# Laying the attention of two transformer layers between the projection units, in groups of two heads

## The reference

```python
xn = rms_norm(h, norm_mix[i]);  mn = rms_norm(mem, norm_mem[i])
mk, mv = halves(mn @ w_mem_kv[i])                  # 4 memory heads
q, k, v, (f_logit), qm = parts(xn @ w_in[i])       # 12 heads of 64; f_logit in layer 0 only
# layer 0 (fox):  s = q.k/8 + F[t] - F[s], F = cumsum(log_sigmoid(f_logit + b)), causal
# layer 1 (moba): one block of 256, so s = q.k/8 - slope[h]*(t-s), causal
# memory heads:   s = qm.mk/8 over 256 memory rows, no mask
h = h + concat(softmax(s) @ v for all 16 heads) @ w_out[i]
h = h + (silu(hn @ w_gate) * (hn @ w_up)) @ w_down[i]     # hn = rms_norm(h, norm_ffn[i]), width 2816
```

## Time and profile before

| | us |
|---|---|
| median of 3 runs | 1815.13 (1812.03 to 1815.88) |
| profiled execution, own time | 1809.4 |
| its span, first to last instruction | 1807.7 |
| TensorE busy | 1595.3 (88%) |
| VectorE busy | 1018.7 (56%) |
| ScalarE busy | 726.1 (40%) |
| mean granted clock of TensorE | 0.932 |

### The profile page before, as it was taken

One profiled execution on the slowest core, in us unless ns is written; L12 is line 12 of the kernel. 1 busy time (PEld: TensorE's weight loads), 2 busy tenths in 40 slices (PEclk: granted clock), 3 DMA queues, 4 the chain that ended last, 5 costly groups with the idle time before them and its releaser, 6 DMA issues.

```text
span 1807.7 us, 23290 instructions
## 1 busy us (share of the span) xinstructions
PE 1595.3 (88%) x7836; PEld 1144.4 (63%) x7836; DVE 1018.7 (56%) x2272; ACT 726.1 (40%) x1750; POOL 513.4 (28%) x573
## 2 busy tenths in 40 slices
PE   5999999999899899997999997888887778777776
PEld 4975789998865799996888786444442223222222
DVE  4443476666654566663335315666666667666644
ACT  4543354444343444443154201434444444444432
POOL 1000000000100000000000001777777776777773
PEclk9975899999975899998999899999999999999999
DMA  7420247664730256662433233999999999999997
GB/s 282 165 92 1 71 152 254 239 249 152 255 118 1 94 198 244 244 220 76 144 110 119 70 140 118 411 410 409 409 409 409 409 409 409 410 409 409 409 410 285
DMA packets 102017, 443.97 MB, mean 246 GB/s; under 512 B 11376, under 2 KB 11648, under 8 KB 84272
## 3 DMA queue, kind: packets, MB, share of 16 engines
q0 software_dynamic: 81632, 297.80, 42.0%
q1 hardware_dynamic: 19584, 141.57, 21.5%
q10 hardware_dynamic: 720, 3.59, 0.5%
HBM read 441.86 MB, written 1.05 MB: 245 GB/s over the span
## 4 chain that ended last, share of the span: by engine, by line
PE 58%; DMA 22%; POOL 9%; DVE 4%; issue 4%; ACT 2%; ACTq 0%; POOLq 0%; DVEq 0%
DMA late<-expert_v,idx 18%; PE PS L400 12%; PE PS L413 7%; PE PS L418 7%; PE PS L422 7%; POOL attn L348 5%; POOL late L356 5%; PE PS L709 4%; PE PS L516 4%; PE PS L489 3%; PE PS L449 3%; PE PS L552 2%; PE PS L556 2%; PE PS L557 2%; DMA attn<-expert_u,idx 2%
## 5 line engine op out<-in xcount | busy, mean ns | idle before, releaser
L709 PE MATMUL PS<-late,wrg 128*128 128x512 f32 x1024 | 500.2, 616 | 130.6 <-DMA late<-expert_v,idx 114.5
L709 PEld LDWEIGHTS PS<-late,wrg 128*128 128x128 f32 x1024 | 177.5, 190 | 439.1 <-DMA late<-expert_v,idx 276.6
L1545 DVE CUSTOM_DVE_ANT_0 attn<-attn,PS 128x1024 f32<-128x1024 f32 x256 | 312.5, 1221 | 238.3 <-DMA attn<-expert_u,idx 238.3
L348 POOL DMA_INDIRECT attn<-expert_u,idx x256 | 241.4, 943 | 380.8 <-DVE idx L1529 300.5
L356 POOL DMA_INDIRECT late<-expert_v,idx x256 | 241.4, 943 | 98.5 <-PE PS L709 54.3
L334 POOL DMA_DIRECT2D ada<-w_ada x46 | 24.4, 530 | 734.2 <-DVE mod L1155 734.2
L1067 DVE TENSOR_TENSOR early_splits<-ring,early_splits 128x1024 fp32r<-128x1024 f32 x132 | 161.6, 1225 | 98.4 <-ACT early_splits L771 92.3
L771 ACT ACTIVATE early_splits<-ring 128x1024 fp32r<-128x1024 f32 x132 | 139.4, 1057 | 150.6 <-PE PS L413 104.2
L400 PE MATMUL PS<-XN,ring 128*128 128x256 f32 x816 | 183.8, 386 | 15.6 <-DVE XN L1376 7.8
L400 PEld LDWEIGHTS PS<-XN,ring 128*128 128x128 f32 x816 | 158.0, 194 | 42.8 <-DVE XN L1376 8.2
L1013 ACT ACTIVATE gel<-dot 128x1 f32<-128x1 f32 x256 | 51.3, 200 | 283.6 <-DVE dot L1545 283.1
(11 more groups left out here) (245 smaller groups left out, 2341.8 us busy)
## 6 DMA issues: line engine op xcount, KB each, us to landing
ring<-wstream SPq DMA_DIRECT2D x134, 1024.0 KB, 4.8
ada<-w_ada POOLq DMA_DIRECT2D x48, 512.0 KB, 3.9
attn<-expert_u,idx POOLq DMA_INDIRECT x256, 17.7
late<-expert_v,idx POOLq DMA_INDIRECT x256, 17.7
con<-const ACTq DMA_DIRECT2D x1, 1168.0 KB, 11.9
MEM<-mem_t ACTq DMA_DIRECT2D x1, 1024.0 KB, 7.7
X<-x_t ACTq DMA_DIRECT2D x1, 1024.0 KB, 9.6
subk<-sub_keys POOLq DMA_DIRECT2D x1, 1024.0 KB, 7.5
```

Of the source, the lines that this page charges most:

```text
L348: gp.indirect_dma_start(UB[i % SLOTS_U], None, expert_u, bass.IndirectOffsetOnAxis(ap=idx[:, n % 3, k:k + 1], axis=0)).then_inc(u_landed[i ...
L709: mm = pe.matmul(PS[:, 2 * b + g, :], DIAG[:, i % 8, :], VB[i % SLOTS_V][:, g * 512:(g + 1) * 512], start=n % 8 == 0 and k == 0, stop=n % ...
L1545: ve.tensor_tensor_reduce(row, row, H2N[n // 8], 1.0, 0.0, ALU.mult, ALU.add, dot[:, n % 2, k:k + 1]).then_inc(dot_ready, 1)
```

## The change

- Order of the units (SP): the stream in HBM stays, but units are loaded singly, in the order of `FUSED`: memory queries, q0, k0, v, then q, k and v in turns, then the output units. A load waits for the unit six before it.
- Attention in 16 groups of two heads and one block of queries. After the projection unit of a step TensorE turns the group before, does the scores of this group, and multiplies the one before with V. The memory heads come first. Both heads' scores lie in banks 4 and 5, both turned parts in bank 6, heads in bank 7. Some steps (`v` units, the last output units) have no new group.
- VectorE does the softmax of the group before it splits the next unit; one maximum and one inversion serve both heads; memory scores aren't copied, the maximum and the exponential read PSUM. The heads' low part is made group by group.
- The first three output units multiply the first six pairs of heads (18 of 24 matmuls), then the last two pairs as these come.
- The sum of squares of X of layer 0 is made at the start; in layer 1 after the first memory key unit, with the other three behind it. The memory split for layer 1 is spread over the feed forward.
- `ada_sum` runs 36 times in feed forward 0 (two a step), 12 times in feed forward 1, never in the projections; `trig` moves to feed forward 1. The residual adds after a feed forward begin as pairs of chunks end (`down_part`). Dummy activations load ScalarE's tables ahead of their use.
- Two small weight loads (wrg, wig) move from the start to the end of feed forward 1.

```diff
+FUSED = (("qm", 0, 0), ("qm", 1, 1), ("q", 0, 1), ("k", 0, 1), ("v", 0, 1), ("v", 1, 0),
+         ("q", 1, 1), ("k", 1, 1), ("q", 2, 1), ("k", 2, 1), ("v", 2, 0), ("v", 3, 0),
+         ("q", 3, 1), ("k", 3, 1), ("q", 4, 1), ("k", 4, 1), ("v", 4, 0), ("v", 5, 0),
+         ("q", 5, 1), ("k", 5, 1), ("wo", 0, 1), ("wo", 1, 1)) + tuple(("wo", c, 0) for c in range(2, KC))
+PAIR_ORDER = (6, 7, 0, 1, 2, 3, 4, 5)
+HELD = 3
+EARLY = 6
 # tensor
+            def group_scores(layer, g):
...
+                for hh, r in enumerate(rows):
+                    mm = pe.matmul(PS[:, 4 + hh, 0:nk], QT[r, pair, b * P:(b + 1) * P], KT[r, pair, 0:nk],
+                                   start=True, stop=not fox)
...
+                        mm = pe.matmul(PS[:, 4 + hh, 0:nk], con[r, c0:c0 + P], FT[r, 0:nk], start=False, stop=True)
+            def attend(layer, before, now):
+                if before is not None:
+                    group_turn(layer, before)
+                if now is not None:
+                    group_scores(layer, now)
+                if before is not None:
+                    group_values(layer, before)
...
+                proj(bank["km", 0], at, mem, (mh_ready, ml_ready))
+                if layer:
+                    norm_sum(NORM_BANK, SQ, KC)
+                proj(bank["km", 1], at + 1, mem)
+                pair_half(bank["vm", 1], at + 2, 0, mem)
+                pair_half(bank["vm", 1], at + 3, 1, mem)
...
+                for s, (kind, c, _) in enumerate(FUSED[:-KC]):
+                    u = FUSED_AT[layer] + s
...
+                    attend(layer, before, group_at[s])
+                    before = group_at[s]
...
+                for c in range(HELD):
...
+                    out_part(bank["wo", c], u, PAIR_ORDER[:EARLY], first=True, signal=c == 0)
+                    attend(layer, before, group_at[s])
 # vector, one step of first_block
+                    if before is not None:
+                        group_tops(layer, before)
+                    if earlier is not None:
+                        group_low(layer, earlier)
+                    if before is not None:
+                        group_normalise(layer, before)
+                    split_lo(FUSED_AT[layer] + s + 2)
 # scalar, one step
+                    if before is not None:
+                        group_exps(layer, before)
+                    split_hi(FUSED_AT[layer] + s + 2)
...
+                        take(KT[:, c, :], tile("k", c))
...
+                    if before is not None:
+                        group_turned(layer, before)
+                        group_heads(layer, before)
 # vector, start of layer 0
+            split_lo(0)
+            chunks_lo(MEML, MN, MEMH, mh_ready, ml_ready)
+            split_lo(1)
+            invert_rms()
+            scale_norm(XN, X, gain("norm_mix0"), RS, normed)
```

More of the change, by code:

```diff
@@ L337, in _ @@
             gp.wait_ge(down_done, 2 * NF)
[L338 removed]
+            for dst, src in ((wuq, w_uq), (wukv, w_ukv), (wrg[:], w_rg), (wig[:], w_ig)):
                 gp.dma_start(dst, src).then_inc(latent_loaded, 16)
@@ new lines, in group_turn @@
+            def group_turn(layer, g):
+                pair, b = groups[g]
+                nk, base = keys_of(pair, b), len(groups) * layer
+                pe.wait_ge(p_ready, base + g + 1)
+                if g >= 1:
+                    pe.wait_ge(pt_copied, base + g)
+                out, probs = halves(6, nk), two(PR, g, nk)
+                for hh in range(2):
+                    for kc in range(nk // P):
+                        mm = pe.transpose(out[:, hh, kc * P:(kc + 1) * P], probs[:, hh, kc * P:(kc + 1) * P], ident)
+                mm.then_inc(pt_ready, 1)
@@ new lines, in group_values @@
+            def group_values(layer, g):
+                pair, b = groups[g]
+                nk, base = keys_of(pair, b), len(groups) * layer
+                pe.wait_ge(pt_copied, base + g + 1)
+                if g >= 1:
+                    pe.wait_ge(heads_lo, base + g)
+                nkc, turned = nk // P, two(PT, g, nk)
+                for hh in range(2):
+                    h = 2 * pair + hh
+                    for kc in range(nkc):
+                        mm = pe.matmul(PS[DH * hh:DH * hh + DH, 7, 0:P], V[:, kc, h * DH:(h + 1) * DH],
+                                       turned[:, hh, kc * P:(kc + 1) * P], start=(kc == 0), stop=(kc == nkc - 1))
+                mm.then_inc(pv_done, 1)
@@ new lines, in group_normalise @@
+            def group_normalise(layer, g):
+                pair, b = groups[g]
+                nk, base = keys_of(pair, b), len(groups) * layer
+                a = 2 * (g % 2)
+                ve.wait_ge(exp_done, base + g + 1)
+                ve.reciprocal(rsum[:, a:a + 2], ssum[:, a:a + 2]).then_inc(vec_step, one(vec_step))
+                ve.wait_ge(vec_step, own(vec_step))
+                probs = two(PR, g, nk)
+                for hh in range(2):
+                    ins = ve.tensor_scalar(probs[:, hh, :], probs[:, hh, :], rsum[:, a + hh:a + hh + 1], None, ALU.mult)
+                ins.then_inc(p_ready, 1)
@@ L1188, in feed_forward @@
                 product_lo(1, 1, False)
+                if layer == 0:
+                    scale_norm(MN, MEM, gain("norm_mem1"), RM, mem_normed, range(4, KC))
+                    ve.wait_ge(c_ready, due(c_ready))
+                else:
+                    trig(0, 1)
                 u += 5
+                loops = (NF - 4) // 2
                 steps = own(vec_step)
[L1191 to L1199 removed]
@@ new lines, in feed_forward @@
+                u += 3 * (NF - 4)
+                for f in (NF - 2, NF - 1):
+                    split_lo(u)
+                    split_lo(u + 1)
+                    product(f, f % 2, True)
+                    split_lo(u + 2)
+                    product_lo(f, f % 2, True)
+                    if layer == 0:
+                        half = KC // 2 * (f % 2)
+                        chunks_lo(MEML, MN, MEMH, mh_ready, ml_ready, range(half, half + KC // 2))
+                    else:
+                        trig(1, f % 2)
+                    u += 3
```

883 lines of the change are left out of this document (511 added, 372 removed).

## The result

The changed kernel took **1817.94 us** (median; 1815.54 to 1821.26), the kernel before 1809.23 (1803.41 to 1815.88) on the same chip: ratio **1.0043**, 95% interval 1.0032 to 1.0054. It is 0.4% slower; 1712 was forecast, in a range of 1688 to 1772. The profiled execution took 1816.62 us, its span is 1815.0, against 1809.4 and 1807.7.

The account below looks back on a forecast made before the run. Low-clock TensorE was taken to bound attention. Gains of 3.6 + 45.4 + 6.1 + 49.8 + 0.5 less 2 make 103.4; 1809.4 - 103.4 = 1706, plus 5.7 gives 1712 us, range 1688 to 1772.

Parts of the forecast that it names:

- What bounds the kernel: Attention stages, 89.48 and 74.29 us: bound by TensorE at its lower level, 1.2 GHz, mean clock 0.54.
- The rival with a low clock in the pieces: Fused stages: clock low in attention pieces, units at full speed; 1776 us; chance 0.16, fully or in part.
- the one that loses by it: Fused stages: low clock takes the 55 units too, 5.1 in place of 2.88 us each; 1898 us; chance 0.04.
- Layer 0: Start wins 3.6 us (0 to 6); from there to the norm 130.6 against 176.0 us, 45.4 won.
- Attention between units: Attention pieces between projection units, at full clock: 40 us in layer 0, 34 us in layer 1.
- New waits: Fused stages: TensorE waits for softmax and PSUM copies, 8.5 us a layer, plus 1.5 for layer 0's table loads.
- Layer 1: Start wins 6.1 us (3 to 7); then 120.3 against 170.1 us, 49.8 won.
- What is moved into the feed forward: Feed forward 0: one more ada_sum a step fits VectorE's idle time; 2 us booked (0 to 20).
- if feed forward 0 is longer than 200: Sign in the profile after that the forecast is wrong; feed forward 0 was expected to take 194 to 196 us.
- no change: Whole kernel: time stays the same, only by a cost of the same size elsewhere; chance 0.01.
- the one for the ada sums: Feed forward 0: VectorE or loads 1 us late a step, 18 steps, 1728 us; chance inside the forecast's 0.62.
- The 5.7 us that I carried along: Whole kernel: the median of runs (1815.1) lies 5.7 us above the profiled execution, added to 1706 for 1712.

Follow-up runs that it names:

- head by head: The kernel with the lead, but in layer 0 each head's score and forgetting product follow each other, as before the change: 1699.82 us.
- The kernel with the lead: The changed kernel with both feed forwards' unit splits issued two units further ahead on ScalarE and VectorE: 1702.98 us, ratio 0.943.
- a lead of one: The changed kernel with its feed forward splits one unit further ahead on ScalarE and VectorE: 1711.55 us, ratio 0.9435.

## Why the prediction was wrong, step by step

- **What bounds the kernel.** Right for attention: it was the low clock, and laying it between full-speed units ends that (0.99 in both fused stages; the forecast was above 0.95). The rival with a low clock in the pieces, and the one that loses by it, didn't come.
- **Layer 0.** Start: the unit behind the gate begins at 46.1; 41.3 to 44.2, with low clock 45.5, was forecast, and 3.0 of the 3.6 were won. The memory unit waited 3.6 us for its split, then ran at low clock (4.5 us). Fused: 125.94 us against 130.6.
- **Attention between units.** 40 and 34 us were booked: too much, and this is a term that was mis-sized, if not the one that decided. Taken out of the fused stages, it took 125.94 - 80.6 (28 units) - 10.9 (waits) = 34.4 and 118.96 - 77.8 - 10.4 = 30.8. What was mis-sized is the pieces for two heads: in the rows above, eight instructions of scores over 256 keys take 1.06 us (105.36 to 106.42), where I booked 1.54 + 0.13, and four of values 0.37 (106.42 to 106.79), where I booked 0.58. At my 0.107 for each 128 columns eight instructions one by one would take 1.7, so the heads run side by side throughout. I had read the one start 0.04 apart in the earlier trace rows as an exception, "only one such start in eight"; with the two rows that are missing there (shown with the experiment on head by head) the heads run side by side in the kernel before too, the second begun 0.58 us later, and the 1.54 us that I took as the price has this late start in it. A change over still costs what I took, 0.1: the two turns from 105.05 to 105.36 are 0.31. The Trainium skill says in TensorEngine Tiling (Array Packing), Key Properties, that tiles work independently of each other; I had set that aside, and these rows agree with it. Of the drain at a change of mode, which the same section names, they show no more than that 0.1.
- **New waits.** 10 and 8.5 booked, 10.9 and 10.4 measured. They stand where they were forecast in kind (turns for VectorE, values for ScalarE's copy); the norm's wait for the last residual add, 2.2 and 2.5, and one of 2.0 at a held-back output unit, were not among them. Turns wait 7 and 4 times in 16 groups, by 0.6 on average; every second group was too many. The 1.5 us for table loads around the forget gate don't show as a wait of TensorE. So 4.2 and 4.5 us of what was measured weren't in my sum and about as much of my sum didn't come: that the totals agree is partly luck.
- **Layer 1.** 137.86 us from its start to its norm; 18.9 + 120.3 = 139.2 forecast.
- **What is moved into the feed forward: the step that failed.** I booked 2 us (0 to 20) and wrote "Step time 8.64". I took this step time as given, weighed whether one more ada sum fits in VectorE's idle time, and found that it does (26.5 us of it "ahead of one split in three"). That reading is right where the lead is two units: there the doubled sums cost nothing that can be seen. But I took the order of the splits in the feed forward for unchanged, because the loop's body is, and never asked which unit a split in the loop is for. The full diff of the two kernels has it: splits ahead of the loop go, the base of `u` changes, three splits come behind the last step. Measured in place of the 2 us: +63.4 and +50.7, from 41 waits of 2 us for the down unit's low part and the lower clock behind some of them. My own sign of being wrong, "if feed forward 0 is longer than 200", came, and so did the case "no change", for which I had seen "only a cost of the same size elsewhere" and "no mechanism".
- **The range.** Only one of my rivals was a wait of TensorE in a feed forward: the one for the ada sums, "1 us late a step: 18 steps, 1728". It had one of the two stages, the wrong cause and less than a third of the size: the wait is 2 us, in both feed forwards, and nine and five times it brings the lower clock. The 5.7 us that I carried along from three executions were too much as well: 15 executions of the kernel before have a median of 1809.2, its profiled one took 1809.4.

Everything but this step makes 1809.4 - 110.3 + 3.4 (norms and rest), 1702.5 for the profiled execution, where 1706 was forecast. The kernel with the lead is at 1695 in its own, the fastest of its four (median 1703), with feed forward 1 at 191.4. So with the lead there the rest of the forecast comes out, though by errors that cancel in part: the start and layer 1 gave 5.4 us more than forecast, norms and the rest took 3.4.

## What to carry to other kernels

When a change rewrites the order of an in-order engine's list, count for every stage behind it, changed or not, how many tiles each producer is ahead of the consumer at the stage's first instruction; a loop body that is the same text does something else when it starts two tiles earlier. Look for the instruction in it that waits for the consumer (here `product`), and check what the consumer needs next stands ahead of it. An engine's idle time is room for more work only where that work doesn't stand between such a wait and the consumer's next need, and where two lists are coupled by a ring, look at what stands behind the ring's wait before one of them gets a lead alone: here that made the kernel 59 us slower.

## What the runs showed of the hardware that I had not expected

- A wait of TensorE of 1.97 us, in a stream that is else full, can be paid twice: at 302.10, a microsecond after the restart, the granted clock is 0.50 and stays so for 3.2 us (to 305.30), and then it is 1.00 again. This came after nine of 20 such waits in feed forward 0 and after five of 21 in feed forward 1 (in feed forward 0 a unit then took 4.45 us in place of 2.95). Why after these and not after the others, no run shows. In the kernel with a lead of two, at the same work, there are neither waits nor this, but for one stretch of 3.4 us at each feed forward's start.
- Plain float32 scores of two heads with 64 rows each, on partitions 0 to 63 and 64 to 127, take 1.06 us for eight instructions of 256 columns, and do so in either order of the kernel's text; a pair of heads' values (four instructions, 64 columns of the array each) 0.37.
- The DMA engines went from a share of 0.62 to 0.80 (222 to 274 GB/s) in feed forward 0 with no cost that TensorE felt where the lead was two units: it was busy 192.68 of 193.31 us. VectorE's waits for the ada loads were 7.0 us there, up to 1.6 each, and 11.0 us, up to 2.5, with a lead of one.
